# Splitting 30 more column tiles of the first projection into three fp32r products, with the lower parts made by GpSimd

## The reference, cut to what matters

```python
u = rms_norm(h, w_norm_mix[l])                      # 272 tokens x 1024
proj = jnp.einsum('btd,dk->btk', u, w_in[l])        # conf (a, g) | z | xbc (x) | dt | gates
...
xbc = jax.nn.silu(depthwise_conv(xbc, w_ssm_conv[l], b_ssm_conv[l]))   # 7 taps, 3072 channels
...
y = bidir_ssd(xs, dt_raw, ssm_dt_bias[l], ssm_a_log[l], Bs, Cs, ssm_d[l])
```

## Time and profile before

| | before |
|---|---|
| median of 3 runs (lowest to highest) | 2490.36 us (2490.23 to 2491.74) |
| the profiled execution | 2487.34 us |
| its span in the trace | 2485.6 us |
| TensorE matmul, busy | 2329.1 us (94%) |
| VectorE | 1212.3 us (49%) |
| ScalarE | 724.9 us (29%) |
| GpSimd | 15.1 us (1%), 22 instructions |
| mean granted TensorE clock | 0.972 |

### The profile page before, as it was taken

The page is one execution under the profiler, slowest core; times in us unless marked ns, Lnnn a source line. Parts: engine busy times, 40 slices in busy tenths (PEclk is TensorE's granted clock), DMA queues, the critical chain, the costliest instruction groups (busy, mean ns, idle before and its releaser), DMA issues. The chain is left out here.

```text
span 2485.6 us, 34782 instructions
## 1 busy us (share of the span) xinstructions
PE 2329.1 (94%) x14382; PEld 1584.6 (64%) x14382; DVE 1212.3 (49%) x2476; ACT 724.9 (29%) x1272; POOL 15.1 (1%) x22
## 2 busy tenths in 40 slices
PE   8999999999998888888988889999999999999998
PEld 6787778962232223222322247889999999888887
DVE  5677985621111111111111126158887776788887
ACT  2135566420000000000000013224454444455554
POOL 1000000000000000000000000000000000000000
PEclk9999999999999999999999989999999999999999
DMA  5375555768999999999999973215765555777785
GB/s 166 117 221 173 174 168 171 249 274 363 427 427 429 426 428 428 427 428 427 429 427 428 427 296 119 86 52 176 230 222 173 177 174 185 249 242 240 243 241 163
DMA packets 205452, 677.52 MB, mean 273 GB/s; under 512 B 15072, under 2 KB 137200, under 8 KB 180336
## 3 DMA queue, kind: packets, MB, share of 16 engines
q1 hardware_dynamic: 205296, 675.30, 73.0%
HBM read 657.40 MB, written 17.83 MB: 272 GB/s over the span
## 5 line engine op out<-in xcount | busy, mean ns | idle before, releaser
L1112 PE MATMUL ps<-ring,tokens 128*34 128x512 f32 x1264 | 279.2, 593 | 27.8 <-DMA ring<-in_w_up 20.4
L2158 PE MATMUL ps<-m_hi,row_hi 128*128 128x256 f32 x1024 | 256.4, 288 | 0.8 <-ACT peer_s L2224 0.8
L2158 PE MATMUL ps<-m_lo,row_hi 128*128 128x256 f32 x1024 | 250.7, 283 | 0.0
L605 PE MATMUL ps<-u,ring 128*128 128x272 f32 x1024 | 244.7, 395 | 3.0 <-DVE ring L423 3.0
L605 PEld LDWEIGHTS ps<-u,ring 128*128 128x128 f32 x1024 | 191.5, 190 | 46.2 <-issue 7.2
L1112 PEld LDWEIGHTS ps<-ring,tokens 128*34 128x34 f32 x1264 | 72.1, 112 | 231.6 <-issue 177.3
L1112 PE MATMUL ps<-extra_early,tokens 128*34 128x512 f32 x752 | 194.0, 664 | 20.7 <-DMA extra_early<-in_w_up 13.8
L1259 DVE TENSOR_SCALAR spread<-ps,slot_at 98x272 fp32r<-98x272 f32 x16 | 8.0, 501 | 393.9 <-PE ps L1098 393.9
L1135 PE MATMUL ps<-ring,first_room 128*34 128x512 f32 x752 | 178.9, 627 | 21.9 <-DVE first_room L1277 10.5
L2158 PEld LDWEIGHTS ps<-m_hi,row_hi 128*128 128x128 f32 x1024 | 195.7, 191 | 1.6 <-issue 1.0
L2158 PEld LDWEIGHTS ps<-m_lo,row_hi 128*128 128x128 f32 x1024 | 196.1, 191 | 0.0
(11 more groups left out here) (431 smaller groups left out, 3165.8 us busy)
## 6 DMA issues: line engine op xcount, KB each, us to landing
ring<-in_w_up SPq DMA_DIRECT2D x47, 2048.0 KB, 23.1
ring<-in_w_down SPq DMA_DIRECT2D x47, 2048.0 KB, 24.5
ring<-in_w_gate SPq DMA_DIRECT2D x32, 2048.0 KB, 22.3
extra_early<-in_w_gate SPq DMA_DIRECT2D x31, 2048.0 KB, 21.0
ring<-in_w_in SPq DMA_DIRECT2D x36, 1024.0 KB, 5.4
extra_early<-in_w_up SPq DMA_DIRECT2D x16, 2048.0 KB, 25.1
extra_early<-in_w_down SPq DMA_DIRECT2D x16, 2048.0 KB, 25.7
rows<-in_peer_u SPq DMA_DIRECT2D x64, 512.0 KB, 3.9
```

The lines of the kernel that those rows point to most:

```text
L605: last = pe.matmul(bank[:, 0:T], wt[:, k, c:c + P], s.u[:, k, :], start=k == 0, stop=k == KT - 1)
L1112: last = pe.matmul(ps[HALF * j:HALF * j + CAP, 2 * c + u % 2, :], s.tokens[:, 2 * (u // 2) + k, CAP * i:CAP * i + CAP], rows[k][:, 1024 * ...
L2158: pe.matmul(out, hi[:, P * k:P * k + P], m[:, k, :], start=k == 0 and m is s.m2_hi, stop=False)
```

## The change

Split tiles are now x20 to x23 and x0 to x15 (tiles 5 to 24) and all of a and g, 36 in place of 6. All 36 lower parts are made by GpSimd, one `tensor_tensor` of 128x1024 each, under a semaphore of its own (`w_lo_pool`); the lower parts of later tiles stay with VectorE. The rounded tokens and their lower part are made before the first tile. GpSimd clears `decay` behind its 29th subtraction. ScalarE makes 30 more upper parts, each ahead of the evacuation of two tiles before.

```diff
+X_FIRST = 5
...
-    mid = range(pos["a", 0] + 6, pos["a", 0] + 12)
+    x_parts = list(range(X_FIRST, pos["a", 0]))
+    mid = x_parts + list(range(pos["a", 0], pos["z", 0]))
+    by_pool = len(mid)
...
+    def lower_ready(n):
+        return (w_lo_pool, n + 1) if n < by_pool else (w_lo, n + 1 - by_pool)
...
             pool.memset(s.cb[:, :, :], 0.0).then_inc(masks, 1)
-            pool.wait_ge(cb_out, GROUPS)
-            pool.memset(s.decay[:, :, :], 0.0).then_inc(clean, 1)
+            for n in range(by_pool):
+                pool.wait_ge(w_hi, n + 1)
+                pool.tensor_tensor(weights_of(n, s.t1_lower), weights_of(n), upper_part(n).bitcast(F32), ALU.subtract).then_inc(w_lo_pool, 1)
+                if n == len(x_parts) + 8:
+                    pool.wait_ge(cb_out, GROUPS)
+                    pool.memset(s.decay[:, :, :], 0.0).then_inc(clean, 1)
...
+            dve.wait_ge(u_hi, 1)
+            dve.tensor_tensor(s.u_lo_mid[:, :, :], s.u[:, :, :], s.u_hi_mid[:, :, :].bitcast(F32), ALU.subtract).then_inc(u_lo, 1)
             dve.wait_ge(evac_a, pos["dt", 0] + 1)
...
             conv_ssm([12, 13, 14, 15])
-            dve.wait_ge(u_hi, 1)
-            dve.tensor_tensor(s.u_lo_mid[:, :, :], s.u[:, :, :], s.u_hi_mid[:, :, :].bitcast(F32), ALU.subtract).then_inc(u_lo, 1)
-            for n in range(3):
-                lower_weights(n)
             conv = conv_conf()
             for i in range(CONV_BEFORE):
-                if i % 2 == 1 and 3 + i // 2 < len(mid):
-                    lower_weights(3 + i // 2)
                 next(conv, None)
...
-                        pe.wait_ge(w_lo, n + 1)
+                        pe.wait_ge(*lower_ready(n))
...
                     act.wait_ge(hi_used, n - 1)
-                    act.wait_ge(w_lo, n - 1)
+                    act.wait_ge(*lower_ready(n - 2))
...
             act.activation(s.a_exp[:, :], s.col("a_log"), ACT.Exp).then_inc(aexp, 1)
+            act.wait_ge(normed, KT)
+            act.activation(s.u_hi_mid[:, :, :], s.u[:, :, :], ACT.Copy).then_inc(u_hi, 1)
...
             for t in range(pos["dt", 0] + 1, pos["a", 0]):
+                if t + 2 in mid:
+                    round_weights(parts_of[t + 2][0])
                 evacuate(t)
...
             for i, t in enumerate(range(pos["a", 0], first_pair_tile)):
-                if t == mid[0] - 4:
-                    act.activation(s.u_hi_mid[:, :, :], s.u[:, :, :], ACT.Copy).then_inc(u_hi, 1)
                 if t + 2 in mid:
                     round_weights(parts_of[t + 2][0])
```

More of the change, by code:

```diff
@@ L236, in mixer @@
              "y_mid", "squared", "y_sum", "conf", "centred", "centred2", "scaled", "silu", "gates", "ystd", "merged",
-             "w_hi", "w_lo", "hi_used", "y_hi", "y_lo", "c_hi", "c_lo", "m_hi", "m_lo", "u_hi", "u_lo")
+             "w_hi", "w_lo", "hi_used", "y_hi", "y_lo", "c_hi", "c_lo", "m_hi", "m_lo", "u_hi", "u_lo", "w_lo_pool")
     (init, masks, squared0, sum0, std0, normed, tiled, evac_a, evac_d, neg, exp, w_out, log_out, aexp,
@@ L241, in mixer @@
      y_mid, squared, y_sum, conf_done, centred, centred2, scaled, silus, gates_done, ystd, merged_step,
-     w_hi, w_lo, hi_used, y_hi, y_lo, c_hi, c_lo, m_hi, m_lo, u_hi, u_lo) = (
+     w_hi, w_lo, hi_used, y_hi, y_lo, c_hi, c_lo, m_hi, m_lo, u_hi, u_lo, w_lo_pool) = (
         s.sem(f"mix_{k}") for k in names)
```

## The result

The changed kernel takes 2530.49 us (median of four runs, 2530.26 to 2530.69) against 2490.30 before: 40.2 us more, a ratio of 1.0161 with a 95% interval of 1.0144 to 1.0179. In its profile the first scan pair starts at 238.92 in place of 196.99, 41.9 us late, and the first GpSimd instruction of the expert layers is 42.0 us late too (564.27 in place of 522.30). So everything was lost ahead of the pair loop, and nothing came back. (The zero of a profile moves a little: the first products of `u` with the ring start at 16.43 before, at 15.94 after and between 15.3 and 17.0 in the experiments. So a difference between instants of two profiles is good to about 1.5 us.)

A forecast was written before the change was run, and what follows sets the result against it. TensorE was taken as the bound, VectorE having 25 us of slack. VectorE's 84.4 us of work, 50.4 of subtractions, later steps and clock losses put the scan pair 31.5 us late: 2521 us against 2490.4, range 2469 to 2545.

The forecast's parts named there:

- What a split tile gives: On TensorE's path, a split tile takes 3.10 us in place of 3.69: 0.59 us a tile, 17.7 us for 30.
- the first rival: VectorE and GpSimd run side by side in the convolutions, so the 17.7 us come whole: 2473 us, chance 0.20.
- What is moved at no cost, and the roundings: Before and during the tiles: rounded tokens and their lower part fit gaps, 30 roundings of 1.06 us on ScalarE; cost 0.
- The exclusion: In VectorE's convolutions, its instructions and GpSimd's subtractions exclude each other; each subtraction costs VectorE its whole 2.1 us.
- The duration of a subtraction: On GpSimd, one pass per input over 1024 columns: 2.1 us, with 1.06 and 3.2 us as low and high ends.
- The sum up to the end of the ssm convolution: VectorE from 38.6: 84.4 us own work, 50.4 for 24 subtractions, 1.7 clock; end at 175.1, 32.9 us late.
- Tile i = 6: Behind the ssm convolution ScalarE needs 3.5 us, so this tile starts at 178.6 in place of 151.7, 26.9 us late.
- From there to the scan pair: Conf convolution with five subtractions (10.5 us), then the rest: VectorE last at 226.8, TensorE 222.3; 31.5 us late with clock.
- The clock: TensorE's granted clock falls behind idle time: 1.7 us lost each in the x stage, before the conf convolution and in the loop.
- The second and third rival: Exclusion with a subtraction of 1.06 us, 2487 us, chance 0.07; or of 3.2 us, 2553 us, chance 0.07.
- The fourth: GpSimd, held by VectorE's queue, gets in late and the stop moves to lower-part waits; same sum, 2521, no own chance.

The follow-up runs named there:

- the run with PSUM: The changed kernel, but the 144 ssm convolution instructions read their second input from PSUM (zeros) in place of SBUF; conf convolution untouched: 2495.75 us.
- the memset beside the copy: Two runs of the changed kernel: each of the 36 subtractions made a GpSimd memset, which only writes (2472.47 us), or a copy reading one SBUF input (2506.99 us).

## Why the prediction was right, and where its sizes were off

The direction and the mechanism that decides it hold. The prediction had 31.5 us, the runs show 40.2 (41.9 at the scan pair in the profile). Step by step the account is less good than at its end: errors of both signs cancel on the way, and one instant agrees by luck.

- **What a split tile gives**, 0.59 us: held. Where nothing on GpSimd reads, all 30 together gave 16.4 us of the 17.7 predicted (one execution), and the first rival's time of 2473 is what that version takes (2472.5). As a rival for the change itself it falls.
- **What is moved at no cost, and the roundings**: held, by the same run.
- **The exclusion**, the step on which the sign hung: shown. It was argued from a memset that held a `tensor_scalar`; the case that decides, two SBUF inputs against a GpSimd instruction that reads SBUF, is shown by the run with PSUM and by the memset beside the copy, which take away one side each. The bare memset of `decay`, 2.80 us by the prediction's estimate, took 2.83 in the changed kernel, where VectorE stood still.
- **The duration of a subtraction**: 2.36 to 2.42 us where it is free, in place of 2.1 from the selects. The Trainium skill's figure (GPSIMD Engine Reference, section 3.1), 2.25 as an estimate, is nearer; the measurement is 5 to 8% above it.
- **The sum up to the end of the ssm convolution**: 175.1 predicted, 170.2 measured. VectorE's six convolutions took 112.1 us in place of 68.4 (from the rows of L362 and L365), 43.7 for the 21 subtractions that fell into them, 2.1 each. 24 were counted, with 50.4 us. Against this the first convolution started 1.6 us later than assumed and the four mask groups took 16.9 us in place of 14.6, so errors of both signs are in the 5 us.
- **Tile i = 6**: 178.6 predicted, 179.1 measured, and that is luck. The prediction had TensorE idle from 165 to 178 behind ScalarE, which waits for the end of the convolution. TensorE was busy 14.6 of 15.0 us from 164 to 179 and did not wait for the silu at all. It had lost its time before, in three waits for lower parts (6.0, 5.3 and 4.6 us), in two for VectorE (13.0 and 3.9 us) and by the lower clock behind them. With stops in the ssm convolution the predicted wait is there: 13.6 us, up to 183.1.
- **From there to the scan pair**: 48.2 us predicted, 59.8 measured. This is where the sum went wrong. The prediction let the five subtractions cut into the conf convolution and called the case in which VectorE holds GpSimd out "a variant of the forecast", with the same sum. It is not the same. VectorE went through its row at full speed (18.23 us for 44), which helped nobody, and TensorE stood 13.6 us with its lower part unmade and all its later tiles still to come. The prediction had TensorE at the scan pair 4.5 us ahead of VectorE. Here VectorE, its row long done, stood 14.3 us for ScalarE, whose work stands behind TensorE's `rows(0)`:

```profile
233.70 1.29 DVE L404 TENSOR_TENSOR ring<-ring,cb 128x1088 f32<-128x1088 f32 x1 [14.29 <-ACT ring L853]
```

- **The clock**: three losses of 1.7 us predicted, 5.1 in all, and some 12 us measured, from TensorE's busy time above. Granted clocks of 0.50 for some 4 us and 0.81 for 4 more stand behind the 13.6 us wait alone (2.8 us lost), and the mean of the stage was 0.86. TensorE stood still in more places than the sum knew of (6.0, 3.9, 13.0, 5.3, 4.6 and 13.6 us, and 1.6 and 1.7).
- **The second and third rival** fall with the duration: 2.4 us is neither 1.06 nor 3.2, and what one subtraction took from VectorE is 2.1. **The fourth**, which was given no chance of its own, describes the x stage and the conf convolution as they ran, but not with the same sum.

## What to carry to other kernels

A GpSimd instruction that reads SBUF was free here only where VectorE ran nothing with two SBUF inputs, and no `tensor_scalar` in SBUF either. Otherwise it cost VectorE about what it takes itself, or GpSimd waited, mostly until VectorE stopped for itself. So look at the timeline of VectorE, not at GpSimd's busy share, place each such instruction behind an event of VectorE's own (here the end of a mask group), and where VectorE has no gap, let it do the work itself (1.23 us a part here, against 2.1). When you find that two engines exclude each other, ask in both directions who is held, since a wait of the engine that bounds the kernel counts in full, and time taken from an engine with slack need not count at all.

## What the runs showed of the hardware that I had not expected

- A GpSimd instruction that reads SBUF can be held out by a row of 40 VectorE instructions, not by one: 16 us (18.72 less 2.4), and 8 us in rows of 20. With VectorE stopping after every four instructions the longest of 36 subtractions took 2.69 us.
- In the first row of all (43.63 to 64.5) the roles were the other way round: subtractions asked for 0.4 to 0.6 us behind the last one got in at once (2.4 to 2.6 us each) and VectorE's row took twice its time. Those asked for 1.9 us or more behind the last one, beside a row, were held out. The pause alone does not decide: in the run with PSUM one asked for 2.5 us behind the last one, 0.3 us ahead of the conf convolution's row of two-input instructions, got in at once (2.6 us), and in the changed kernel one asked for 0.2 us ahead of such a row (65.52) was held. What decides was not tested.
- A TensorE idle time of 11 us was followed by 8 us at a granted clock of 0.50, which took back about half of what moving the scan pair 7.7 us forward had won.
- A memset on GpSimd, which only writes, held no two-input instruction of VectorE, but it did hold a one-input `tensor_scalar`: 3.13 us beside the memset of `decay`, and four times 0.71 to 0.84 us in place of 0.42 beside the short ones.
